# Gated delta rule: inverse begun with an 8 by 8 block inverse by powers, and key, query and value products made once for two units

## What is computed

```python
decay = jnp.exp(jnp.where(causal, gc[..., :, None] - gc[..., None, :], -jnp.inf))
kb = k * beta[..., None]
lower = jnp.where(strict, jnp.einsum('nhcid,nhcjd->nhcij', kb, k) * decay, 0.0)
rhs = jnp.concatenate([v * beta[..., None], kb * jnp.exp(gc)[..., None]], axis=-1)
uw = lax.linalg.triangular_solve(lower, rhs, left_side=True, lower=True, unit_diagonal=True)
...
def step(state, inp):
    u_c, w_c, qk_c, qg_c, kd_c, a_c = inp
    v_new = u_c - jnp.einsum('nhik,nhkv->nhiv', w_c, state)
    o = jnp.einsum('nhik,nhkv->nhiv', qg_c, state) + jnp.einsum('nhij,nhjv->nhiv', qk_c, v_new)
    state = state * a_c[..., None, None] + jnp.einsum('nhjk,nhjv->nhkv', kd_c, v_new)
    return state, o
```

## Time and profile before

| | |
|---|---|
| median of 3 runs | 3282.64 us (3277.35 to 3283.25) |
| profiled execution, its own time | 3281.89 us |
| its span | 3280.1 us |
| TensorE busy in the span | 3077.8 us (94%) |
| VectorE, ScalarE, POOL busy | 1353.9, 1131.0, 1545.2 us |
| mean granted TensorE clock | 0.973 |
| delta core: first matmul, first inverse, last output added | 678.55, 685.93, 1026.7 us |

### The profile page before, as it was taken

The page is one execution under the profiler, slowest core; times in us unless marked ns, Lnnn a source line. Parts: engine busy times, 40 slices in busy tenths (PEclk is TensorE's granted clock), DMA queues, the critical chain, the costliest instruction groups (busy, mean ns, idle before and its releaser), DMA issues.

```text
span 3280.1 us, 56094 instructions
## 1 busy us (share of the span) xinstructions
PE 3077.8 (94%) x23316; PEld 2683.6 (82%) x23316; DVE 1353.9 (41%) x2522; ACT 1131.0 (34%) x1753; POOL 1545.2 (47%) x1191
## 2 busy tenths in 40 slices
PE   6999999999998899999999979898999999999998
PEld 4787778888887677787778867798987999987998
DVE  3221347655554421234222356424455552455452
ACT  2222223322222222222222244433454564444563
POOL 1444444411112344443445441487872688563686
PEclk8999999999999899999999989999999999999899
DMA  7434322210000344433432231254542455341453
GB/s 298 167 122 166 126 88 102 81 37 2 2 3 17 127 144 147 163 126 137 150 113 103 84 109 35 78 183 141 190 150 69 141 173 186 130 162 59 140 175 131
DMA packets 58923, 390.16 MB, mean 119 GB/s; under 512 B 6480, under 2 KB 7760, under 8 KB 21360
## 3 DMA queue, kind: packets, MB, share of 16 engines
q1 hardware_dynamic: 49472, 322.07, 28.4%
q10 hardware_dynamic: 9072, 64.25, 5.7%
q0 software_dynamic: 192, 1.18, 0.1%
HBM read 386.42 MB, written 1.05 MB: 118 GB/s over the span
## 4 chain that ended last, share of the span: by engine, by line
PE 62%; POOL 18%; issue 13%; DVE 4%; ACT 2%; DMA 0%; POOLq 0%; ACTq 0%; DVEq 0%
POOL ring_lo L2487 18%; PE bank L637 15%; PE bank L638 15%; PE bank L639 15%; PE bank L672 2%; PE bank L1174 1%; PE bank L890 1%; PE bank L893 1%; PE bank L878 1%; DVE core L2394 1%; PE bank L1079 1%; PE bank L1185 1%; PE bank L699 1%; PE bank L1067 1%; PE bank L817 0%
## 5 line engine op out<-in xcount | busy, mean ns | idle before, releaser
L2487 POOL TENSOR_TENSOR ring_lo<-ring,w_hi 128x512 fp32r<-128x512 f32 (+1 forms) x832 | 1093.8, 1345 | 1241.9 <-ACT w_hi L1331 1241.5
L639 PE MATMUL bank<-h_hi,ring_lo 128*128 128x256 f32 (+1 forms) x3384 | 1118.9, 331 | 0.0
L637 PE MATMUL bank<-h_hi,w_hi 128*128 128x512 f32 (+1 forms) x2448 | 864.9, 353 | 52.0 <-POOL ring_lo L2487 29.0
L638 PE MATMUL bank<-h_lo,w_hi 128*128 128x512 f32 (+1 forms) x2448 | 850.0, 347 | 0.0
L639 PEld LDWEIGHTS bank<-h_hi,ring_lo 128*128 128x128 f32 x3384 | 653.4, 193 | 59.6 <-issue 0.5
L637 PEld LDWEIGHTS bank<-h_hi,w_hi 128*128 128x128 f32 x2448 | 470.1, 192 | 130.8 <-issue 50.6
L1331 ACT ACTIVATE w_hi<-ring 128x2048 fp32r<-128x2048 f32 (+2 forms) x226 | 395.2, 1749 | 411.6 <-PE bank L639 325.8
L638 PEld LDWEIGHTS bank<-h_lo,w_hi 128*128 128x128 f32 x2448 | 471.0, 192 | 52.9
L639 PE MATMUL bank<-hid_r,ring_lo 128*128 128x256 f32 (+1 forms) x1088 | 364.3, 335 | 0.0
L1925 DVE SCALAR_TENSOR_TENSOR core<-core,bank 128x512 f32<-128x512 f32 (+1 forms) x88 | 54.6, 621 | 653.5 <-ACT core L1399 653.5
L637 PE MATMUL bank<-hid_r,w_hi 128*128 128x512 f32 (+1 forms) x808 | 289.9, 359 | 2.3 <-POOL ring_lo L2487 2.3
(11 more groups left out here) (392 smaller groups left out, 4496.0 us busy)
## 6 DMA issues: line engine op xcount, KB each, us to landing
ring<-w SPq DMA_DIRECT2D x88, 1024.0 KB, 4.9
zbuf<-ada_later ACTq DMA_DIRECT2D x60, 1024.0 KB, 4.8
ring<-up SPq DMA_DIRECT2D x48, 1024.0 KB, 4.8
ring<-w SPq DMA_DIRECT2D x64, 704.0 KB, 4.1
ring<-mla_in SPq DMA_DIRECT2D x24, 1024.0 KB, 4.8
ring<-down SPq DMA_DIRECT2D x32, 768.0 KB, 4.3
ring<-dn_in SPq DMA_DIRECT2D x16, 1024.0 KB, 4.8
ring<-ada SPq DMA_DIRECT2D x12, 1024.0 KB, 12.2
```

The source lines that it names most:

```text
L637: pe.matmul(out, a[0], b[0], start=start, stop=False)
L638: pe.matmul(out, a[0], b[1], start=False, stop=False)
L639: return pe.matmul(out, a[1], b[0], start=False, stop=stop)
L2487: ins = pool.tensor_tensor(like(ring_lo[:, r, a:b], part), like(ring[:, r, a:b], part), part.bitcast(F32), ALU.subtract)
```

## The change

The six levels become four stages: an inverse of the 8 by 8 blocks on the diagonal, by powers, and three levels with blocks of 8, 16 and 32. With N the negated strictly triangular part of an 8 by 8 block, (1 + N)(1 + N²)(1 + N⁴) is the inverse. `turned_blocks` makes the transpose of the triangular matrix, `masked` at n = 0 keeps the 8 by 8 blocks of it, `near_blocks` (VectorE) keeps them of the matrix itself, `near_identity` (POOL) adds the identity, `squares` makes N² and its transpose, `squares_out` (ScalarE) takes them out, `fourths` makes N⁴ and the product of N² with (1 + N), `fourths_out` (VectorE) adds, `diagonals` multiplies the two factors, and `diagonals_out` (ScalarE) takes out X and XT.

Second, `value_turn`, `key_key` and `key_query` run only for even units. `keep_keys` and `keep_queries` (ScalarE) copy the products of keys and queries to SBUF at places that are free in those units (`raw_home`), and `lower`, `query_decay` and `residual` of an odd unit read what the other stream had in the unit before.

```diff
-LEVELS = 6
+LEVELS = 4
+DIAG = 8
...
         for n in range(LEVELS):
-            m = 1 << n
+            m = DIAG << n >> 1
...
+            if n == 0:
+                full = -1.0 * ((a // DIAG == b // DIAG) & (a > b))
...
+                def squares(U, s):
+                    q = quad[s]
+                    pe.wait_ge(dn["ym"][s], 5 * U + 2)
+                    if U >= 1:
+                        pe.wait_ge(dn["outd"][s], U)
+                    for hd in range(QUAD):
+                        for r in HALVES:
+                            pe.matmul(small4(s, C1, 0)[r, hd, :], q["NT"][r, hd, :], q["YL"][r, hd, :], start=True, stop=True)
+                    for hd in range(QUAD):
+                        for r in HALVES:
+                            mm = pe.matmul(small4(s, C1, 1)[r, hd, :], q["YL"][r, hd, :], q["NT"][r, hd, :], start=True, stop=True)
+                    mm.then_inc(dn["z"][s], 1)
+
+                def fourths(U, s):
+                    q = quad[s]
+                    pe.wait_ge(dn["inv"][s], 5 * U + 1)
+                    pe.wait_ge(dn["qdm"][s], 2 * U + 1)
...
                 def updates(U, n, s):
...
-                        for r in HALVES:
-                            pe.matmul(small4(s, C1, 0)[r, hd, :], xt(r, hd), q["YL"][r, hd, :], start=True, stop=True)
...
+                        for r in HALVES if n < LEVELS - 1 else (SEEN[s],):
+                            pe.matmul(small4(s, C1, 0)[r, hd, :], q["XT"][r, hd, :], q["YL"][r, hd, :], start=True, stop=True)
...
                 for U in range(UNITS_D):
                     more = U + 1 < UNITS_D
-                    for n in range(LEVELS):
...
+                    fresh = more and U % 2 == 1
+                    for s in range(2):
+                        turned_blocks(U, s)
+                    for s in range(2):
+                        key_state(U, s)
+                    for s in range(2):
+                        squares(U, s)
+                    for s in range(2):
+                        key_turn(U, s)
+                    for s in range(2):
+                        fourths(U, s)
...
+                def keep_keys(U, s):
+                    act.wait_ge(dn["lt"][s], U + 1)
+                    act.activation(raw_home(0, U, s), dbank[s][A0], ACT.Copy).then_inc(dn["raw"][s], 1)
+
+                def keep_queries(U, s):
+                    act.wait_ge(dn["qd"][s], U + 1)
+                    act.activation(raw_home(1, U, s), dbank[s][A1], ACT.Copy).then_inc(dn["raw"][s], 1)
+
+                def squares_out(U, s):
+                    act.wait_ge(dn["z"][s], 6 * U + 1)
+                    act.activation(quad[s]["XX"].rearrange("p h t -> p (h t)"), dwide[s][C1][:, :], ACT.Copy).then_inc(dn["inv"][s], 1)
...
+                def near_blocks(U, s):
+                    q = quad[s]
+                    dve.wait_ge(dn["lt"][s], U + 1)
+                    for r in HALVES:
+                        ins = dve.tensor_tensor(q["NT"][r, :, :], q[f"LT{U % 2}"][r, :, r],
+                                                level(1 - s, 0)[r, :].unsqueeze(1).broadcast_to([64, QUAD, 64]), ALU.mult)
+                    ins.then_inc(dn["ym"][s], 1)
...
+                def fourths_out(U, s):
+                    q = quad[s]
+                    dve.wait_ge(dn["y"][s], 7 * U + 2)
+                    dve.tensor_tensor(q["X"], small4(s, C0, 0), identc.unsqueeze(1).broadcast_to([P, QUAD, 64]), ALU.add)
+                    dve.tensor_tensor(q["XT"], small4(s, C0, 1), q["NTI"], ALU.add).then_inc(dn["xu"][s], 1)
...
+                def near_identity(U, s):
+                    q = quad[s]
+                    pool.wait_ge(dn["ym"][s], 5 * U + 1)
+                    pool.tensor_tensor(q["NTI"], q["NT"], identc.unsqueeze(1).broadcast_to([P, QUAD, 64]), ALU.add).then_inc(dn["qdm"][s], 1)
```

More of the change, by code:

```diff
@@ L400, in out_block, with raw_home @@
             return v[:, hg * QUAD:hg * QUAD + QUAD, tc * CK:(tc + 1) * CK]
+        def raw_home(part, U, s):
+            c = 2 * part + s
+            v = h[:, QUAD + c, :] if U < 4 else qkv[:, DNH + c, :]
+            return v.rearrange("p (h t) -> p h t", h=QUAD)
         def edge_col(U, s, hd=0, n=1):
@@ new lines, in diagonals @@
+                def diagonals(U, s):
+                    q = quad[s]
+                    pe.wait_ge(dn["xu"][s], 4 * U + 1)
+                    for hd in range(QUAD):
+                        for r in HALVES:
+                            pe.matmul(small4(s, C1, 0)[r, hd, :], q["XT"][r, hd, :], q["X"][r, hd, :], start=True, stop=True)
+                    for hd in range(QUAD):
+                        for r in HALVES:
+                            mm = pe.matmul(small4(s, C1, 1)[r, hd, :], q["X"][r, hd, :], q["XT"][r, hd, :], start=True, stop=True)
+                    mm.then_inc(dn["z"][s], 1)
@@ L945, in delta_core @@
                     more = U + 1 < UNITS_D
-                    for n in range(LEVELS):
+                    fresh = more and U % 2 == 1
[9 more added lines that the diff above has]
+                        fourths(U, s)
+                    if more:
+                        for s in range(2):
+                            decay_row(U + 1, s)
+                    for s in range(2):
+                        diagonals(U, s)
+                    if fresh:
+                        for s in range(2):
+                            value_turn(U + 1, s)
+                    for n in range(1, LEVELS):
                         for s in range(2):
@@ L949, in delta_core @@
                         for s in range(2):
-                            if n == 0:
-                                key_state(U, s)
-                                key_turn(U, s)
-                            elif n == 1 and more:
-                                decay_row(U + 1, s)
-                            elif n == 2 and more:
-                                value_turn(U + 1, s)
-                            elif n == 3 and U % 2 == 0 and U > 0:
+                            if n == 1 and U % 2 == 0 and U > 0:
                                 head_sums(U - 1, s)
-                            elif n == 4 and more:
+                            elif n == 2 and fresh:
                                 key_key(U + 1, s)
@@ L1764, in delta_core_act @@
                 act.wait_ge(gates_done, 2)
-                for part in (decay_mat, values_in):
+                for part in (decay_mat, values_in, keep_keys, keep_queries):
                     for s in range(2):
@@ L1769, in delta_core_act @@
                     more = U + 1 < UNITS_D
+                    fresh = more and U % 2 == 1
+                    for part in (squares_out, key_decay):
+                        for s in range(2):
+                            part(U, s)
+                    if more:
+                        for s in range(2):
+                            decay_exp(U + 1, s)
                     for s in range(2):
-                        key_decay(U, s)
+                        diagonals_out(U, s)
                     if U % 2 == 0 and U > 0:
@@ L1775, in delta_core_act @@
                     if more:
-                        for part in (decay_exp, decay_mat, values_in):
+                        for s in range(2):
+                            decay_mat(U + 1, s)
+                    if fresh:
+                        for part in (values_in, keep_keys):
                             for s in range(2):
@@ L1781, in delta_core_act @@
                             part(U, s)
+                    if fresh:
+                        for s in range(2):
+                            keep_queries(U + 1, s)
             act.wait_ge(x_in, 16)
@@ L2421, in delta_core_dve @@
                     dve.memset(quad[s]["XTF"], 0.0)
-                for part in (decay_gap, lower, query_decay):
+                for part in (decay_gap, lower, near_blocks, query_decay):
                     for s in range(2):
@@ L2517, in head_gate @@
                     pool.tensor_tensor(block, block, out_block(zs, U, s), ALU.mult).then_inc(hz_done, 1)
+                for s in range(2):
+                    near_identity(0, s)
                 for U in range(UNITS_D):
@@ L2525, in delta @@
                             head_gate(U - 1, s)
+                    if U + 1 < UNITS_D:
+                        for s in range(2):
+                            near_identity(U + 1, s)
                 for s in range(2):
```

169 lines of the change are left out of this document (106 added, 63 removed).

## The result

The changed kernel takes 3243.90 us (median of 4 runs, 3237.69 to 3247.64), the kernel before in the same session 3279.99 us: a ratio of 0.988 (0.9862 to 0.9898), 1.2% less. A second series gave 3239.86 and 0.9874 (0.9853 to 0.9895). The forecast was 3230, with a range of 3216 to 3250.

The account below looks back on a forecast made before the run. The prediction took the unbroken TensorE and VectorE chain through the delta core (first inverse to last output) as the bound. Its eight units sum to 288.1 us against 340.8, 52.7 less: 3281.9 - 52.7 = 3229.2, said as 3230, range 3216 to 3250.

Parts of the forecast that it names:

- its own case: Whole kernel: the core's units shrink from 340.8 to 288.1 us; time 3218 to 3240, chance 0.72.
- rival (a): In the core, handoffs and clock falls (2.4 to 1.2 GHz) take back 10 to 28 us: 3240 to 3257; chance 0.16.
- the walk: Step-by-step timeline of the core's new units, both streams followed through TensorE's queue and data; sums to 288.1 us.
- No wait before `fourths` and `diagonals`: In the new inverse, `squares_out` and `fourths_out` finish before TensorE arrives at 7.05 and 11.04 us from unit start.
- ScalarE's queue: Ahead of `diagonals_out`, the `key_decay` and `decay_exp` work ends by 11.7 us, before products at 12.23; no delay.
- costed at nothing: `near_identity` on POOL, `near_blocks` and the next unit's `query_decay` on VectorE lie in free places of the core: no cost.
- step 7 of the walk: From `new_values` to the next unit: 8.01 us with `next_state` or S in the outputs, 6.2 in units 0, 3, 4.
- granted clock of 0.5 in more than two places: Sign that the forecast is wrong: TensorE's clock halved at more than two places of the core.
- the other signs: Right: first inverse about 686 us, last output near 974. Wrong: the stretch behind the core longer than 2253 us.
- Rival (b): The removed products in the core were only cover, so their 19 us don't come: 3249; chance 0.07.
- Zero for half of the last updates: Last level's `updates` drop 4 of 16 matmuls, all of one array half: 0 us taken, 3.7 by count.
- The slower rival (c): TensorE stays at 1.2 GHz in the core; gain gone after 53 us of such work, 3340 with three units; chance 0.03.

Follow-up runs that it names:

- after_again: The changed kernel run once more with no edit; 3239.86 us, ratio 0.9874 to the kernel before.
- cover4_early: On cover4, in unit 0 `query_decay` moved behind the first `masked` on VectorE and `keep_queries` behind `squares_out` on ScalarE; 3235.20 us, ratio 0.9857.
- cover4: The changed kernel plus four 128x128 products nobody reads (the cover), behind `join` in units without `key_query`; 3230.59 us, ratio 0.9847.
- only_shared: The kernel before, keeping its six levels, with the three products made only for even units and copied; 3265.34 us, ratio 0.9947.
- cover8_before_join: The changed kernel with eight thrown-away products of both streams ahead of `join`, in units without `key_query`; 3224.74 us (one run).
- full_last: On cover4, the last level's updates made on both halves of the array again, as before the change; 3234.02 us (one run).
- cover_small: The changed kernel with a cover of sixteen thrown-away 64x64 products instead of four of 128x128; 3231.08 us (one run).
- only_inverse: The changed kernel with `value_turn`, `key_key` and `key_query` made in every unit and nothing kept in SBUF; 3247.63 us, ratio 0.9897.
- split: The changed kernel with the two `inverse` copies of stream 1 made by VectorE instead of ScalarE; 3229.29 us, ratio 0.9846.
- split_cover4: The changed kernel with both split's VectorE copies and cover4's four thrown-away products; 3229.02 us, ratio 0.983.
- split_cover2: The changed kernel with split's VectorE copies and a cover of two thrown-away 128x128 products instead of four; 3232.26 us, ratio 0.9824.

## Why the prediction was right, and where it was too high

**Right in the range, and not by its own case.** The forecast was 3230, and its own case, which has no price for falls in the joins, ended at 3240. The measured 3243.90 lies above that, in the 3240 to 3257 of rival (a), and the second series, 3239.86, at the edge. The range held because it reached into (a), and it was (a)'s mechanism that took part of the gain back.

**The forecast was 52.7 us, the profiled execution gave 38.2.** The 14.5 us between them are: 5.0 and 2.2 outside the core, which lie within the scatter of the profiles; 7.4 in the tails of the five joins, the clock; 1.6 in the prologue (from the first `decay_row` to the first `turned_blocks`), where the clock fell within the first `decay_row` (below 1.00 from 682 to 686 us; the pair is recorded at 2.42 us, 2.02 before; 8.94 us to the first `turned_blocks` against 7.38). The place was chance, the loss was not: in after_again and in every other kernel with the new inverse except cover4_early the fall came a little later, behind the wait of 2.31 us before the first `squares`, and the way to the first `new_values` was as long (36.5 us in the changed kernel, in after_again and in cover4). Elsewhere the walk had about 1.7 too much. These last two cancel, which is luck: with the cover, and so without the 7.4, the core gave 348.2 - 295.4 = 52.8 us.

**The walk to `new_values` was right to half a microsecond.** From each unit's start to `new_values` it gave 27.3, 31.9, 29.6, 29.8, 27.6, 31.9, 29.6 and 22.9 us. Measured: 27.6, 31.7, 29.1, 29.6, 27.3, 31.7, 29.1, 22.7 (717.29 - 689.71 in unit 0, 942.71 - 913.57 in unit 6).

**No wait before `fourths` and `diagonals`; ScalarE's queue.** As forecast. The copies that weren't in the trace of before take 0.60 (forecast 0.59), and the near blocks and the identity lie where nothing waits, except at the start of unit 0. Groups of the changed kernel in the core:

```profile
L2476 DVE TENSOR_TENSOR near<-core,con 64x256 f32<-64x256 f32 x32 | 16.9, 528 | 0.5
L2640 POOL TENSOR_TENSOR near<-near,con 128x256 f32<-128x256 f32 x16 | 15.5, 966 | 161.6 <-DVE near L2476 161.6
...
L1825 ACT ACTIVATE core<-bank 128x512 f32<-128x512 f32 x16 | 9.6, 597 | 55.7 <-PE bank L902 55.7
L1829 ACT ACTIVATE core<-bank 128x512 f32<-128x512 f32 x16 | 9.6, 597 | 11.9 <-PE bank L925 11.9
...
L2488 DVE TENSOR_TENSOR core<-h,core 128x512 f32<-128x512 f32 x4 | 3.7, 957 | 0.1
```

`near_blocks` is longer than the 0.4 I took (0.53), `near_identity` 0.97 instead of half of 1.29, and `query_decay` from SBUF 0.96 on average (0.69 and 1.22 by turns) where from PSUM it is 0.69. All of it was costed at nothing outside unit 0, and cost nothing there; in unit 0 `squares` began 3.46 us after `turned_blocks` (689.71 to 693.17) instead of 2.9.

**The step that was off: "from `new_values` to the next unit", taken over from before at 8.01 and 6.2.** This is step 7 of the walk. It measured 8.43, 9.04, 7.18, 10.15 in units 0, 2, 4, 6 and 7.99 in unit 7, where 6.2, 8.01, 6.2, 8.01 and 6.96 stood: 2.2 + 1.0 + 1.0 + 2.1 + 1.0 = 7.4 us too little. In units 1 and 5, with `key_query`, it is 8.02. The cover took exactly these 7.4 us out: in cover4 the five stretches are 6.2, 8.0, 6.2, 8.0 and 7.0 us, so that the values taken over were right for a clock at 1.00, and wrong was that it would stay there. I had this mechanism as rival (a), with one fall at 1.5 us, and gave it 0.16, because before the change the clock stood at 1.00 in the one join that has no product. That was one case. With the new inverse it took place in all five joins without a product, in both profiles; with the six levels of before only in one of only_shared's five. The forecast "granted clock of 0.5 in more than two places" was the sign of error, and it came. Of the other signs, the first inverse began at 689.7 us instead of about 686, the last output came at 983.55 instead of near 974, and the stretch behind the core was longer than 2253 us in the first profile (2258.4) and shorter in the second (2248.0).

**The price of the two parts.** Rival (b), products as mere cover, is refuted: the sharing alone gave 16.8 with one fall of the clock, and the inverse alone 34.1 (forecast 19 and 35). That eight products of the size of `key_query`, at its place, cost 0.6 us and not 1.98 is shown by cover8_before_join. Zero for half of the last updates is shown by full_last; the Trainium skill's statement ("TensorEngine Tiling (Array Packing)", Key Properties) that different tiles multiply in parallel agrees with it, 295.5 against 295.4 us.

**The slower rival (c)** had the right sign of mechanism and was far from its point: the falls together took 9 us of the 53 needed. The Trainium skill's rule that activity releases the clock ("TensorE: Matmul & The Clock Gate", Part 1) agrees in kind, five joins at 0.5 and none once they had work; but four of only_shared's five joins kept the clock behind the same wait.

**What stays open.** What decides between a fall and none at a given join: not the size of the products in it (cover_small), and not the last gap alone (0.45 with a fall, 0.54 without). Why four joins of only_shared (units 0, 4, 6, 7) and unit 7 of only_inverse and of the kernel before were spared wasn't settled. The moment at which the standstill comes is a rival that no run separates: no kernel shifts a join in time and leaves it as it is otherwise, and the joins of split and cover_small lie at different times (`new_values` of unit 0 comes 35.6 and 36.5 us after the core's start). That a cover removes the falls in the joins is shown in all eight kernels that have one; four of these (cover4_early, split_cover4, split_cover2, cover8_before_join) had one or two falls behind `head_sums` instead, at 1.1 to 1.5 us each, as only_inverse and the kernel before had one in unit 2. Why these and not the others stays open too.

## What to carry to other kernels

When a change takes a product out of a stretch in which TensorE waits for another engine, price the clock as well as the product: here the four joins that lost `key_query` gained 0.6 us each by the count and lost 1.0 to 2.2 us each to the work behind them at 1.2 GHz. Work that is thrown away, placed where TensorE would stand still and short enough to end before the wait does, cost nothing here and gave back 7.4 us. And where the code outside the change is untouched, compare the changed stretch in the traces: it repeated within 0.1 us, while the stretch behind it differed by up to 18 from profile to profile.

## What the runs showed of the hardware

- One fall of the clock cost 1.0 to 2.2 us here, where the profile of before had one of 1.5; the two that cost over 2 (units 0 and 6 of the changed kernel) lasted about twice as long as the others. And the place differs from kernel to kernel: where falls in the joins or at the first `squares` had gone, others came at places that had none in cover4 (cover4_early, split_cover2).
- Two halves of the array in turn (16 records of 64x64, 0.68 us) take the time of one half alone (8 records, 0.68), and 12 or 16 matmuls of 64x64 in a stream's last update make no difference (cores of 295.4 and 295.5 us).
- In the changed kernel VectorE's product of two SBUF tiles of 128x512 took 0.69 and 1.22 us by turns (0.96 on average), with POOL at work on SBUF tiles beside both, and 0.69 with one of them in PSUM. What makes the second one longer isn't shown.
